# Suffix sums of a stick-breaking sample group as twelve small matmuls instead of four wide ones, and one weight load moved behind a gate write

## The reference, cut to what matters

```python
z = einsum('bqhd,bkhd->bhqk', q, k) * D ** -0.5 + bias
mask = k_pos < q_pos
log_keep = where(mask, log_sigmoid(-z), 0.0)
after = cumsum(log_keep, axis=3, reverse=True) - log_keep   # all later keys
a = where(mask, exp(log_sigmoid(z) + after), 0.0)
o = einsum('bhqk,bkhd->bqhd', a, v)
...
merged = sigmoid(gate_r) * (ret_branch @ w_ret_proj) + sigmoid(gate_s) * (sb_branch @ w_sb_proj)
h = x + merged @ w_out
```

## Time and profile before

| | us |
|---|---|
| median of three runs | 2078.22 |
| the profiled execution, its own time | 2078.73 |
| its span in the profile | 2076.9 |
| PE busy | 2047.0 (99%) |
| DVE busy | 1505.4 (72%) |
| ACT busy | 980.9 (47%) |
| POOL busy | 114.7 (6%) |

### The profile page before, as it was taken

One profiled execution on the slowest core, in us unless ns is written; L12 is line 12 of the kernel. 1 busy time (PEld: TensorE's weight loads), 2 busy tenths in 40 slices (PEclk: granted clock), 3 DMA queues, 4 the chain that ended last, 5 costly groups with the idle time before them and its releaser, 6 DMA issues.

```text
span 2076.9 us, 42089 instructions
## 1 busy us (share of the span) xinstructions
PE 2047.0 (99%) x15520; PEld 1973.1 (95%) x15520; DVE 1505.4 (72%) x1990; ACT 980.9 (47%) x1419; POOL 114.7 (6%) x109
## 2 busy tenths in 40 slices
PE   8999999999999999999999999999999999999996
PEld 6999999999999999999999999999999999999996
DVE  6976767777772377878878788788787765468876
ACT  5545545446563345444454444544465542234443
POOL 0012211122200000000000000000000000000000
PEclk8999999999999999999999999999999999999998
DMA  5455555555554444333334234343446345543444
GB/s 156 131 137 152 145 149 147 144 148 143 147 162 139 139 122 140 101 97 117 114 113 131 83 116 128 96 119 111 126 127 215 116 155 166 169 149 110 111 126 142
DMA packets 456804, 277.30 MB, mean 134 GB/s; under 512 B 20740, under 2 KB 436868, under 8 KB 455556
## 3 DMA queue, kind: packets, MB, share of 16 engines
q1 hardware_dynamic: 454532, 271.30, 44.3%
q10 hardware_dynamic: 2176, 4.72, 0.6%
HBM read 235.84 MB, written 40.11 MB: 133 GB/s over the span
## 4 chain that ended last, share of the span: by engine, by line
PE 92%; DVE 3%; DMA 1%; DVEq 1%; ACT 1%; issue 1%; ACTq 0%; SPq 0%
PE ACC L780 43%; PE ACC L786 21%; PE ACC L686 14%; PE Z L706 4%; PE Z L834 1%; PE Z L1006 1%; PE Z L914 1%; PE Z L847 1%; PE Z L893 1%; PE Z L816 1%; PE ACC L732 1%; DMA RAW<-in_w_ret_proj 1%; PE Z L1015 1%; PE Z L1081 1%; PE Z L990 1%
## 5 line engine op out<-in xcount | busy, mean ns | idle before, releaser
L1274 ACT ACTIVATE HI<-RAW 128x1024 fp32r<-128x1024 f32 x434 | 448.0, 1053 | 579.2 <-DVEq L1825 288.5
L1802 DVE TENSOR_TENSOR LO<-RAW,HI 128x1024 fp32r<-128x1024 f32 x434 | 534.0, 1239 | 195.6 <-ACT HI L1274 164.7
L780 PE MATMUL ACC<-XH,HI 128*128 128x288 f32 x1728 | 470.8, 298 | 0.9 <-ACT HI L1274 0.9
L780 PE MATMUL ACC<-XL,HI 128*128 128x288 f32 x1728 | 464.3, 295 | 0.0
L780 PE MATMUL ACC<-TH,HI 128*128 128x288 f32 x1296 | 360.0, 303 | 0.0
L780 PE MATMUL ACC<-TL,HI 128*128 128x288 f32 x1296 | 353.0, 297 | 0.0
L780 PEld LDWEIGHTS ACC<-XH,HI 128*128 128x128 f32 x1728 | 324.6, 188 | 14.8 <-issue 14.6
L780 PEld LDWEIGHTS ACC<-XL,HI 128*128 128x128 f32 x1728 | 324.3, 188 | 0.2
L786 PE MATMUL ACC<-XH,LO 128*128 128x288 f32 x1728 | 264.0, 294 | 0.0
L780 PEld LDWEIGHTS ACC<-TH,HI 128*128 128x128 f32 x1296 | 243.8, 188 | 3.3 <-ACT HI L1274 1.2
L780 PEld LDWEIGHTS ACC<-TL,HI 128*128 128x128 f32 x1296 | 243.9, 188 | 0.2
(11 more groups left out here) (340 smaller groups left out, 3092.7 us busy)
## 6 DMA issues: line engine op xcount, KB each, us to landing
RAW<-in_w_in SPq DMA_DIRECT2D x224, 512.0 KB, 4.0
RAW<-in_w_out SPq DMA_DIRECT2D x33, 512.0 KB, 4.2
KV<-in_cache_sb_k SPq DMA_DIRECT2D x256, 64.0 KB, 1.9
KV<-in_cache_sb_v SPq DMA_DIRECT2D x256, 64.0 KB, 1.9
RAW<-in_w_ret_proj SPq DMA_DIRECT2D x32, 512.0 KB, 4.2
RAW<-in_w_sb_proj SPq DMA_DIRECT2D x16, 512.0 KB, 3.9
ST<-in_state_ret SPq DMA_DIRECT2D x64, 128.0 KB, 2.9
out<-ST SPq DMA_DIRECT2D x64, 128.0 KB, 3.6
```

The source lines that it names most:

```text
L780: mm = pe.matmul(to, HI[:, w, k, :], x[:, k, :], start=k == 0 and x is xh, stop=False)
L1274: act.activation(HI[:, SLOT[pos]], RAW[:, SRC[n]], ACT.Copy).then_inc(S["hi_made"], 1)
L1802: dve.tensor_tensor(LO[:, SLOT[pos]], RAW[:, SRC[n]], HI[:, SLOT[pos]].bitcast(F32), ALU.subtract)\
```

## The change: what it does

First, the suffix sums. DVE no longer adds up later pages. ACT and DVE leave log_keep as 320 columns (4 pages of 64 and the new keys), in a high and a low part. PE does for each part: the triangular matrix on 256 columns; the ones matrix with page 3 broadcast over three pages, page 2 over two, page 1 over one (192, 128 and 64 columns); the ones matrix (64 rows) with the new keys broadcast over four pages (256 columns). Two matmuls of 64 rows, 64 weight columns and 64 columns then make the new keys' own sums. On PE, first head, the place behind product 9 (`LO__80` is the operand `LO_`, `MATSR` the two matrices, `Z` the PSUM bank); before:

```diff
@@ sync: first loads of the retention projection
             weights(w_ret[0], 8 * P, 1)
-            weights(w_ret[0], P, 0)
             gates_out(d_gr, 14, RG, 1)
             sp.wait_ge(S["g_out1"], 16 * 8)
             merge_in(8, 1)
-            weights(w_ret[0], P, 1)
-            weights(w_ret[0], 9 * P, 0)
-            weights(w_ret[0], 9 * P, 1)
-            merges(1)
...
-            with sp.Fori(2, 4) as i:
+            with sp.Fori(1, 4) as i:
@@ tensor: q == 9
-                    for m, part in ((0, 0), (1, 0), (1, 512), (0, 512)):
-                        mm = pe.matmul(Z[3][:, 64 * m:320], MATSR[:, m, :], LO_[:, part + 192 * (1 - m):part + 512 - 256 * m],
-                                       start=m == 0 and part == 0, stop=m == 0 and part == 512)
+                    for low in range(2):
+                        part = LO_[:, low * 320:(low + 1) * 320]
+                        pe.matmul(Z[3][:, 0:256], MATSR[:, 0, :], part[:, 0:256], start=low == 0, stop=False)
+                        for c in (3, 2, 1):
+                            pe.matmul(Z[3][:, 0:c * NS].rearrange("p (o n) -> p o n", o=c), MATSR[:, 1, :],
+                                      one(part[:, c * NS:(c + 1) * NS]).broadcast_to([P, c, NS]), start=False, stop=False)
+                        pe.matmul(Z[3][:, 0:256].rearrange("p (o n) -> p o n", o=4), MATSR[0:NS, 1, :],
+                                  one(part[0:NS, 256:320]).broadcast_to([NS, 4, NS]), start=False, stop=low == 1)
+                    for low in range(2):
+                        part = LO_[:, low * 320:(low + 1) * 320]
+                        mm = pe.matmul(Z[3][0:NS, 256:256 + NS], MATSR[0:NS, 0, 0:NS], part[0:NS, 256:320],
+                                       start=low == 0, stop=low == 1)
@@ scalar: n == 9, and the new place of the copy
+                    weights_of(2)
                     logits_back(1)
                     act.drain()
                     softplus(ZS0, ZW, 1)
-                    weights_of(2)
-                    t.take("s_masked")
-                    act.activation(LO_[:, 512:1024], LL[:, 0:512], ACT.Copy).then_inc(S["lh_done"], 1)
...
+            def sample_high():
+                t.take("s_masked")
+                act.activation(LO_[:, 0:320], LL[:, ZS0:ZW], ACT.Copy).then_inc(S["lh_done"], 1)
...
-                        if first and 7 * u + n == 2:
-                            act.wait_ge(S["zz_set"], 1)
...
-                    pair(dst, nothing, after, first and u == 0, 1 if first and u == 0 else 0)
+                    pair(dst, (nothing, sample_high)[u], after, first and u == 0, 1 if first and u == 0 else 0)
...
                 if q == 15:
                     evacuate(1, VG[:, 1, :])
+                    act.wait_ge(S["zz_set"], 1)
@@ vector: n == 9
-                    dve.scalar_tensor_tensor(LL[:, 256:512], ZZ[:, ZS0:ZN0], 0.0, LL[:, ZS0:ZN0], ALU.max, ALU.add)
-                    dve.scalar_tensor_tensor(LL[:, 192:256], ZZ[:, ZN0:ZW], 0.0, LL[:, ZN0:ZW], ALU.max, ALU.add)
+                    dve.scalar_tensor_tensor(LL[:, ZS0:ZW], ZZ[:, ZS0:ZW], 0.0, LL[:, ZS0:ZW], ALU.max, ALU.add)
                     dve.drain()
-                    dve.tensor_tensor(LL[:, 192:256], LL[:, 192:256], KEEP[:, 0, :], ALU.mult)
-                    for c in (2, 1, 0):
-                        dve.drain()
-                        ins = dve.tensor_tensor(LL[:, c * NS:(c + 1) * NS], ..., ALU.add)
-                    ins.then_inc(S["s_masked"], 1)
+                    dve.tensor_tensor(LL[0:NS, ZN0:ZW], LL[0:NS, ZN0:ZW], KEEP[0:NS, 0, :], ALU.mult)\
+                        .then_inc(S["s_masked"], 1)
...
-                    dve.tensor_tensor(LO_[:, 0:512], LL[:, 0:512], LO_[:, 512:1024].bitcast(F32), ALU.subtract)\
+                    dve.tensor_tensor(LO_[:, 320:640], LL[:, ZS0:ZW], LO_[:, 0:320].bitcast(F32), ALU.subtract)\
                         .then_inc(S["ls_low"], 1)
```

More of the change, by code:

```diff
@@ L580, in merge_in @@
                     sp.dma_start(MGI[:, s, k, :], src[c]).then_inc(S[f"mg_in{s}"], 16)
[L582 to L586, removed]
             weights(w_ret[0], 8 * P, 0)
@@ L605, in couple @@
                     weights(w_ret[0], (i + 8 * k) * P, 1)
-                merges(i)
-            with sp.Fori(2, 4) as i:
-                t.enter(i, 2, PER_C)
+                for k in range(2):
+                    t.take("mg_used")
+                    merge_in(i + 8 * k, k)
+            with sp.Fori(1, 4) as i:
+                t.enter(i, 1, PER_C)
                 couple(i)
-                t.leave(2)
+                t.leave(3)
             couple(4)
@@ L1944, in sb_attention @@
                     t.take("w_ln")
-                    dve.scalar_tensor_tensor(LL[:, 256:512], ZZ[:, ZS0:ZN0], 0.0, LL[:, ZS0:ZN0], ALU.max, ALU.add)
-                    dve.scalar_tensor_tensor(LL[:, 192:256], ZZ[:, ZN0:ZW], 0.0, LL[:, ZN0:ZW], ALU.max, ALU.add)
+                    dve.scalar_tensor_tensor(LL[:, ZS0:ZW], ZZ[:, ZS0:ZW], 0.0, LL[:, ZS0:ZW], ALU.max, ALU.add)
                     dve.drain()
-                    dve.tensor_tensor(LL[:, 192:256], LL[:, 192:256], KEEP[:, 0, :], ALU.mult)
-                    for c in (2, 1, 0):
-                        dve.drain()
-                        ins = dve.tensor_tensor(LL[:, c * NS:(c + 1) * NS], LL[:, 320 + c * NS:320 + (c + 1) * NS],
-                                                LL[:, (c + 1) * NS:(c + 2) * NS], ALU.add)
-                    ins.then_inc(S["s_masked"], 1)
+                    dve.tensor_tensor(LL[0:NS, ZN0:ZW], LL[0:NS, ZN0:ZW], KEEP[0:NS, 0, :], ALU.mult)\
+                        .then_inc(S["s_masked"], 1)
                     t.take("sig_made")
@@ L1962, in sb_attention @@
                     t.take("z_dve3")
-                    dve.tensor_tensor(ZZ[:, ZS0:ZN0], ZZ[:, ZS0:ZN0], Z[3][:, 64:320], ALU.subtract)
-                    dve.tensor_tensor(ZZ[0:NS, ZN0:ZW], ZZ[0:NS, ZN0:ZW], Z[3][0:NS, 0:NS], ALU.subtract)
+                    dve.tensor_tensor(ZZ[:, ZS0:ZN0], ZZ[:, ZS0:ZN0], Z[3][:, 0:256], ALU.subtract)
+                    dve.tensor_tensor(ZZ[0:NS, ZN0:ZW], ZZ[0:NS, ZN0:ZW], Z[3][0:NS, 256:256 + NS], ALU.subtract)
                     dve.drain().then_inc(S["z_read3"], 1)
```

## The result

| | before | after |
|---|---|---|
| median, us | 2078.47 (2075.09 to 2078.97, 4 runs) | 2100.02 (2098.06 to 2102.45, 4 runs) |
| profiled execution, its span | 2078.73, 2076.9 | 2102.06, 2100.2 |

The account below looks back on a forecast made before the run. PE, busy 99% of the span, was taken to bound the kernel. Terms 5.5 + 1.6 + 1.5 + 3.3 + 1.5 = 13.4 us put the median at 2091.6 us, from 2078.22; range 2085 to 2097.

Parts of the forecast that it names:

- Suffix sums: Suffix sums on PE: twelve matmuls take 1.21 us instead of 0.52, 0.69 more a head, 5.5 us for eight.
- Order on ACT in ordinary heads: Ordinary heads: softplus now waits for POOL, but about 1 us of slack remains before PE's suffix sums; costs nothing.
- Last head: Last head: PE waits for ACT and DVE ahead of the suffix sums, product 10 starts later; 1.6 us more.
- rival of two falls: Clock falls at the retention load and again in the last head, at 577; 2093 us, chance 0.10.
- First head: First head: ACT's later work delays the evacuation of keys 0, and PE waits for that bank; 1.5 us.
- Just in time: First head: hi(1) is ready at 92.3, and PE starts product 1 at 92.48, so no wait there.
- Load: Retention projection: column block 1 lands late, PE stalls 3.6 us at its ninth quarter, less an old 0.3 wait; 3.3 us.
- The clock: Retention projection, at 1690: the load stall brings TensorE to half rate once; 1.5 us.
- DVE-paced rival: DVE, not PE, paces the heads, so its lighter work makes the kernel faster; 2073 us, chance 0.03.

Follow-up runs that it names:

- e5_rows: Kernel after with all twelve suffix matmuls on 128 rows, the two small ones with 128 weight columns too; 2092.29 us, ratio 1.0072.
- e6_grouped: Kernel after with the suffix matmuls reordered, the eight on 128 rows first, then the four on 64 rows; 2097.31 us, ratio 1.0092.
- e3_act: Kernel before with ACT's order alone changed: hi(2) ahead of the gate softplus, the sample's high-part copy behind hi(3); 2083.59 us, ratio 1.0023.
- e9_fillers: Kernel after with 44 overwritten matmuls added where PE idles, in the last head and ahead of the retention projection's ninth quarter; 2096.45 us, ratio 1.0085.
- e4_zz: Kernel before with only ACT's wait for zz_set moved, ahead of hi(1) of the first head; 2080.09 us, ratio 1.001.
- e2_load: Kernel before with SP's order alone changed: retention column block 1 loaded behind the gate's write and the reads; 2082.38 us, ratio 1.0021.
- e1_suffix: Kernel before with only the suffix sums changed: twelve short matmuls, gate logs in 320 columns, no DVE additions; 2089.24 us, ratio 1.0052.
- e10_warm: Kernel before with 3 times 12 overwritten matmuls added in PE's idle places ahead of token tiles 1 to 3; 2079.08 us, ratio 1.0005.

## Why the prediction failed

**Suffix sums, 5.5 us: mis-sized, the step that failed.** Measured 1.33 a head, 10.6 for eight. The prediction gave each of the ten matmuls with 128 weight columns the 0.105 us of L834, "ten of them take 1.05 us", and 0.08 to each of the two small ones. It put nothing for a change between weights of 128 rows and of 64 and nothing at the product behind. The ten took 1.57 us, the two 0.09 together, the product behind 0.19 more. The price of a short matmul among its like held (0.085 to 0.10 us); with all of them on 128 rows the head is 0.8 us longer, near the 0.69 forecast, and the other 0.5 goes with the changes of rows (e5_rows, e6_grouped). Before's trace hinted at the last part: product 1, behind L851's narrower weights, had 2.33 for its HI part, and the product behind L900's full ones 2.14. The Trainium skill (TensorE: Matmul & The Clock Gate, LDWEIGHTS) has the weight load go by columns and not by rows. The load itself does so here, 0.18 us for 64 rows and 0.19 for 128 in the rows; whether it is hidden does not. The 0.105 that the prediction set beside this rule is how far apart short matmuls start, not how long a load lasts. The same page (Step-by-step: what each phase is for) says that a load is pulled ahead when row groups don't conflict or it goes to the background buffer; the rows show it pulled ahead between weights of 128 rows, and not where the rows change.

**Order on ACT in ordinary heads, nothing: right.** 1.3 us of slack for 1 forecast. e3_act showed how thin that was: with the additions kept it is below nothing.

**Last head, 1.6 us: right, and wrong in what follows.** PE stood 2.5 us for 2.2 forecast. Without the clock, as e9_fillers shows, the head takes 2.18 us more than an ordinary one (66.79 for 64.61); before it was 0.61 (63.89 for 63.28), so the new order adds 1.57. The clock fell here too; the rival of two falls, given 0.10, is what happened in the profiled execution.

**First head, 1.5 us: right as a chain, 2.3 from product 0.** The 1.5 is there when counted from DVE's memset. "Just in time" failed for product 1, as PE came earlier than ACT in this execution. e4_zz alone gave 1.8.

**Load, 3.3 us: mis-sized by 0.7 in this profile, the other way in others.** The stall was 4.3, less the 0.3. Landing was about half a us quicker than taken; what lengthened the stall was a later issue, 1.1 us of it from an earlier load that landed in 4.90 us, where before and in the other runs with the load in its new place (e2_load, e5_rows, e6_grouped, e9_fillers) it took 3.84 to 3.94. The stalls of e2_load, e5_rows and e6_grouped were 2.8, 2.4 and 2.5.

**The clock, 1.5 us: the other step that failed, in number and in price.** The sum had one fall at 1.5 us; the profile has two, at 3.0 and 2.6. The price was read from the first tile, which had begun long after the fall and so showed only what was left of the cold stretch. From the start of dense work a fall cost 1.5 us (e3_act in its last head, e6_grouped at the load), 2.6 and 3.0 (after).

By the profiled spans: start -1.2 (product 0 came earlier, with nothing changed ahead of it), first head 2.3, seven heads 9.3, last head 5.9 (1.3 for the sums, 1.6 for the wait, 3.0 for the clock), the rest up to the retention projection 0.4 (16.8 late at its start), load and clock there 6.9 less 0.3: 23.3. The suffix sums and the clock were short by 5.1 and 4.1 us, which is nearly all of the 9.9 between the 13.4 forecast and the 23.3. The DVE-paced rival is refuted by e1_suffix; DVE's shorter work gained nothing by itself.

## What to carry to other kernels

Price a short matmul with its neighbours: going to weights of fewer rows and back cost 0.1 to 0.2 us each way, and padding them to 128 rows with zeros was cheaper here by 0.49 us a head. Where an edit makes PE stand still for 2.5 us or more in dense work, add a clock fall to the wait, at 1.5 to 3 us, as a likely case. And before filling idle time, look at what releases the work behind it: in the last head filling paid, at the start of the kernel it did not.

## What was not expected of the hardware

A gap of about the same length goes either way. In the last head the clock fell after 2.50 us (after), 2.49 (e6_grouped) and 2.85 (e3_act), and held after 2.49 (e5_rows); at the load it fell after 4.27 (after) and 2.49 (e6_grouped), and held after 2.8 (e2_load) and 2.4 (e5_rows). Gaps of 0.7 to 1.6 among dense products did it in no profile here, but 0.7 to 1.0 among short transposes did (e10_warm). What decides is open. It also means that a median over few executions mixes both.

The pace of PE's matmuls isn't fixed by the granted clock alone. The 1152 matmuls from the ninth quarter on took 153.87 us in the profiled executions of e5_rows and e9_fillers, with the clock at 1.00; in that of e2_load they took 150.05, for the same work at the same clock (its row stands under e2_load). That is 0.130 us a matmul instead of 0.134, 2.5% less. It gives back 3.8 us in this one stage and so hides the whole stall in that execution, which took no longer than the kernel before; the other stages kept the usual pace. Why is open.
